# Moving the low parts of gate and up from GpSimd to VectorE in the steps with several token groups

## What is computed

```python
def swiglu(h, w_in, w_out):
    gate, up = jnp.split(h @ w_in, 2, axis=-1)
    return (jax.nn.silu(gate) * up) @ w_out
# x = x + g2 * rms_norm(swiglu(h, ffn_w_in, ffn_w_out), ffn_post_g);  D_FF = 2816
```

## Time and profile before

| | before |
|---|---|
| median of 3 runs | 2308.24 us (2305.38 to 2310.96) |
| the profiled execution's own time | 2305.82 us |
| span of the profile (first to last instruction) | 2304.0 us |
| PE busy | 2247.8 us, 98% of the span |
| DVE busy | 1358.1 us, 59% |
| ACT busy | 865.5 us, 38% |
| POOL busy | 713.5 us, 31% |
| mean granted clock of PE | 0.994 of full speed |

### The profile page before, as it was taken

The page is one execution under the profiler, slowest core; times in us unless marked ns, Lnnn a source line. Parts: engine busy times, 40 slices in busy tenths (PEclk is TensorE's granted clock), DMA queues, the critical chain, the costliest instruction groups (busy, mean ns, idle before and its releaser), DMA issues.

```text
span 2304.0 us, 31766 instructions
## 1 busy us (share of the span) xinstructions
PE 2247.8 (98%) x12964; PEld 2192.4 (95%) x12964; DVE 1358.1 (59%) x2273; ACT 865.5 (38%) x1200; POOL 713.5 (31%) x310
## 2 busy tenths in 40 slices
PE   8999999999999999999999999999999999999998
PEld 4988889999999999999999999999999999999998
DVE  4688864676757656533556668768365244443246
ACT  3577771454211111222343545544434132111234
POOL 3400002453121121332534544542343243221232
PEclk9999999999999999999999999999999999999999
DMA  9322215332323333343343444543343234321323
GB/s 305 104 84 94 94 63 197 120 135 94 126 95 122 99 110 111 125 131 101 110 138 119 150 141 134 178 137 110 101 156 128 74 110 146 110 74 55 101 94 118
DMA packets 211699, 276.13 MB, mean 120 GB/s; under 512 B 4777, under 2 KB 194785, under 8 KB 211041
## 3 DMA queue, kind: packets, MB, share of 16 engines
q1 hardware_dynamic: 183056, 224.36, 29.7%
q10 hardware_dynamic: 26768, 40.30, 5.0%
q0 software_dynamic: 1728, 9.44, 1.0%
HBM read 245.76 MB, written 28.32 MB: 119 GB/s over the span
## 4 chain that ended last, share of the span: by engine, by line
PE 82%; DVE 6%; issue 4%; ACT 3%; POOL 3%; DMA 2%; SPq 0%; ACTq 0%; POOLq 0%; DVEq 0%
PE bank L1011 77%; PE bank L1041 2%; POOL w_lo L2562 1%; DMA raw<-in_l_ffn_w_out 1%; POOL acc L2579 1%; PE bank L1066 1%; DVE mv_lo L2079 1%; DVE y L2042 1%; ACT w_hi L1432 1%; PE bank L1091 1%; DVE pool_sum L2443 1%; DVE hid_lo L2359 0%; DVE wide L2092 0%; DMA mod_stage<-in_l_mod_w 0%; DVE hid L2356 0%
## 5 line engine op out<-in xcount | busy, mean ns | idle before, releaser
L1011 PE MATMUL bank<-mv_hi,w_hi 128*128 128x384 f32 (+2 forms) x2736 | 924.5, 338 | 6.0 <-DVE mv_lo L2174 2.7
L1011 PE MATMUL bank<-mv_lo,w_hi 128*128 128x384 f32 (+2 forms) x2736 | 918.2, 336 | 0.0
L1011 PE MATMUL bank<-mv_hi,w_lo 128*128 128x384 f32 (+2 forms) x2736 | 918.2, 336 | 0.0
L2562 POOL TENSOR_TENSOR w_lo<-raw,w_hi 128x2048 fp32r<-128x2048 f32 x106 | 491.6, 4643 | 1201.5 <-ACT w_hi L1432 1133.2
L1011 PEld LDWEIGHTS bank<-mv_hi,w_hi 128*128 128x128 f32 x2736 | 515.3, 188 | 11.3 <-issue 8.9
L1011 PEld LDWEIGHTS bank<-mv_lo,w_hi 128*128 128x128 f32 x2736 | 515.2, 188 | 0.0
L1011 PEld LDWEIGHTS bank<-mv_hi,w_lo 128*128 128x128 f32 x2736 | 514.8, 188 | 0.0
L1432 ACT ACTIVATE w_hi<-raw 128x2048 fp32r<-128x2048 f32 x159 | 299.4, 1908 | 431.2 <-DMA raw<-in_l_ffn_w_out 237.1
L1011 PE MATMUL bank<-hid_hi,w_hi 128*128 128x384 f32 (+2 forms) x1056 | 361.2, 342 | 13.8 <-DVE hid_lo L2359 12.2
L1011 PE MATMUL bank<-hid_hi,w_lo 128*128 128x384 f32 (+2 forms) x1056 | 356.3, 337 | 0.0
L1011 PE MATMUL bank<-hid_lo,w_hi 128*128 128x384 f32 (+2 forms) x1056 | 356.1, 337 | 0.0
(11 more groups left out here) (156 smaller groups left out, 1837.0 us busy)
## 6 DMA issues: line engine op xcount, KB each, us to landing
raw<-in_l_ffn_w_in SPq DMA_DIRECT2D x92, 1024.0 KB, 5.1
raw<-in_l_ffn_w_out SPq DMA_DIRECT2D x46, 1024.0 KB, 4.9
raw<-in_l_mod_w SPq DMA_DIRECT2D x42, 1024.0 KB, 5.2
residual<-y ACTq DMA_DIRECT2D x10, 1536.0 KB, 7.1
x_old<-residual ACTq DMA_DIRECT2D x10, 1536.0 KB, 7.1
raw<-in_l_w_in SPq DMA_DIRECT2D x8, 1024.0 KB, 5.3
mod_stage<-in_l_mod_w SPq DMA_DIRECT2D x6, 1024.0 KB, 12.1
raw<-in_l_w_out SPq DMA_DIRECT2D x6, 1024.0 KB, 5.1
```

The lines of the kernel that those rows point to most:

```text
L1011: last = pe.matmul(out, w, x, start=start and n == 0, stop=stop and n == len(steps) - 1)
L2562: pool.tensor_tensor(w_lo[:, slot(w), :], raw[:, q % 2, :], w_hi[:, slot(w), :].bitcast(F32), ALU.subtract).then_inc(w_lo_pool, 1)
```

## The change

It edits three places: the list of work, the list of the places of halves, and DVE's program for a step. In a step with several groups that has no case of its own, both low parts of the next step's weights go to DVE: gate's halves behind the adds of m = 5 and m = 7 of the first group, up's behind those of m = 1 and m = 3 of the second. A new list `DOWN_ON_DVE` names the pieces of down whose low part goes to DVE behind the first pair of their step.

```diff
             if own(layer, s) == s:
                 w = WEIGHT["down", layer, s]
                 t += DOWN_LATER if (layer, s) == (0, 0) else 0.0
-                low = ("DVE", 2.2) if w in LAST_SPLITS else ("POOL", SPLIT_LO)
-                work += [("ACT", ("split", w), t, SPLIT_HI), (low[0], ("split", w), t + SPLIT_HI, low[1])]
+                work.append(("ACT", ("split", w), t, SPLIT_HI))
+                if w in DOWN_ON_DVE:
+                    work.append(("DVE", ("split", w), AT["up", PAIR[layer, s, groups[0], 0]] + 2.4, 2.2))
+                elif w in LAST_SPLITS:
+                    work.append(("DVE", ("split", w), t + SPLIT_HI, 2.2))
+                else:
+                    work.append(("POOL", ("split", w), t + SPLIT_HI, SPLIT_LO))
...
-            elif later and len(groups) == 1 and (layer, s) != (0, 0):
-                places[later[1]] = [(groups[-1], 5), (groups[-1], 7)]
+            elif later and (layer, s) != (0, 0):
+                if len(groups) > 1:
+                    places[later[0]] = [(groups[0], 5), (groups[0], 7)]
+                    places[later[1]] = [(groups[1], 1), (groups[1], 3)]
+                else:
+                    places[later[1]] = [(groups[0], 5), (groups[0], 7)]
...
+DOWN_ON_DVE = [WEIGHT["down", layer, s] for layer in range(2) for s in range(len(STEPS[layer]))
+               if own(layer, s) == s and (layer, s) not in STEP_MODS and len(STEPS[layer][s][1]) == NG]
+DOWN_ON_DVE = [w for w in DOWN_ON_DVE if w not in LAST_SPLITS]
...
-ON_DVE = sorted([0, 4, 5, 6, 7, 8, 9, *DVE_SPLITS, *HALVES, *AFTER_POOL, LAST_SPLITS[-1]])
+ON_DVE = sorted([0, 4, 5, 6, 7, 8, 9, *DVE_SPLITS, *HALVES, *AFTER_POOL, *DOWN_ON_DVE, LAST_SPLITS[-1]])
...
                         k = PAIR[layer, s, g, j]
+                        if (g, j, own(layer, s)) == (STEPS[layer][s][1][0], 0, s) and WEIGHT["down", layer, s] in DOWN_ON_DVE:
+                            split(WEIGHT["down", layer, s])
                         if k in SUM_AFTER_PAIR:
```

## The result

Five runs of the changed kernel have a median of 2320.52 us (2316.67 to 2323.89), five of the kernel before, beside them, 2308.89 us (2305.38 to 2310.96). The ratio is 1.005 with a 95% interval of 1.0034 to 1.0065: slower by 11.6 us, where the sum of the forecast was 11.0 (the time put on record was 2318 us, with a range of 2311 to 2326). The profiled execution took 2316.67 us with a span of 2314.9, which is 10.9 us over the span before, at the same mean granted clock, 0.994.

What follows compares the result with a forecast made beforehand. PE's matmuls plus the moments PE stands were taken as the bound, with 82% of the chain of waits. Seven steps at 6.2 us and three with a norm at 4.8 sum to 11.0 us slower: 2318 us, range 2311 to 2326.

Steps and rivals of the forecast that it cites:

- The bank: Out products of the ten steps: a half delays the next add, whose bank PE wants; 0.44 us per costly half.
- quiet step: Seven steps, (0,2) to (0,5), (1,12), (1,19), (1,20), with POOL idle beside the out products: 0.88 us each, 6.2 in all.
- the first late start: At the first half of a step, PE stands 0.33 us for the late add's bank, plus 0.11 of slow restart.
- the second and fourth halves: In each step of the change, these leave the add 0.13 us late, inside the 0.24 allowed: no stall.
- The norm steps: (0,11), (0,16), (1,22), where POOL's sums of squares stretch the halves: 1.6 us a step, 4.8 in all.
- the whole stretch: Upper end for (0,11), (0,16), (1,22): four halves of 1.86 us to the next add, 3.4 us a step, 10.2 in all.
- The rest of the edit: Loads released later, POOL's relief, DVE's added wait: all free; down's load beats ACT's need by 0.9 us.
- The empty list for down: `DOWN_ON_DVE` excludes all six steps with three groups, so it names no piece and down stays on POOL.
- The chains: Norm chains laid out again in following steps; `hid_lo` waits may go or double, -7.8 to +7.8 us, taken as 0.
- Rival 2: Out products of the ten steps: halves are free and POOL's relief counts, leaving a 7.8 us gain, 2300.4; chance 0.04.
- Rival 3: Three steps with a norm: every half at 1.86 us and sums late on PE, 22.4 us in all, 2330; chance 0.12.
- Rival 1: Steps (0,12) to (1,0): norm chains settle better and pay back 7.8 us, 2311.4, no measurable slowdown; chance 0.14.

Runs made afterwards that it cites:

- the up-alone kernel: Changed kernel with gate's low part back on POOL and up's halves behind m = 5 and m = 7 of the last group: 2314.95 us, 1.0029.
- the quarters: Changed kernel with gate's and up's low parts in pieces of 512 columns behind each of eight adds, instead of halves: 2317.69 us, 1.0041.

## Why the prediction was right

**The bank.** Right, and shown: four banks take all of the loss away, with DVE as busy as in the change. The size of a quiet step was forecast at 0.88 us and measured at 0.96 in (0,2), 0.9 to 1.0 in all seven. What was mis-sized is the first late start, 0.43 instead of 0.33: PE started 0.70 us behind the start of the add that it waited for (668.57 less 667.87), where 0.60 had been read, so the slack there was 0.14 and not 0.24. Why is open. Of this 0.03 came back in a quicker restart (0.08 for 0.11); the third half's, 0.34 and 0.11, was met. That the second and fourth halves are free was right.

**The norm steps.** The direction was right, the term a little small: 1.6 us a step was forecast, 2.1, 2.2 and 1.4 are read from late starts, 5.7 for 4.8. All of that is the bank's, for with four banks the out products of these steps take no longer than before; what PE loses behind them is norm work that came earlier and is paid back in part. How the halves meet POOL is seen in the timeline of DVE in (0,11):

```profile
1099.15 1.97 DVE L2129 TENSOR_TENSOR w_lo<-raw,w_hi 128x1024 fp32r<-128x1024 f32 x1
...
1101.99 1.21 DVE L2129 TENSOR_TENSOR w_lo<-raw,w_hi 128x1024 fp32r<-128x1024 f32 x1
...
1104.61 1.67 DVE L2129 TENSOR_TENSOR w_lo<-raw,w_hi 128x1024 fp32r<-128x1024 f32 x1
...
1107.14 1.21 DVE L2129 TENSOR_TENSOR w_lo<-raw,w_hi 128x1024 fp32r<-128x1024 f32 x1
```

POOL adds up squares there from 1097.90 to 1109.24, one sum right behind the other. Two of these sums:

```profile
1099.01 1.03 POOL L2593 TENSOR_TENSOR acc<-acc,wide 128x392 f32<-128x392 f32 x1
...
1104.17 1.03 POOL L2593 TENSOR_TENSOR acc<-acc,wide 128x392 f32<-128x392 f32 x1
```

I had put three halves midway, at 1.5 us to the next add, and a clean fourth. In fact two are stretched and two are clean, though POOL sums beside all four; in (0,16) likewise (2.03 and 1.69 us), and in (1,22) only the third is stretched (1.69). So the mean was about right by luck, and its reason was not: a half isn't stretched by the share of its time in which POOL is busy, it is stretched or it isn't. The times show what decides. A half that begins while a sum runs ends 1.08 us after that sum: the two sums above end at 1100.04 and 1105.20, the halves at 1101.12 and 1106.28. A clean half begins within 0.02 us of a sum's end, and then the sum behind it is the longer one (2.02 and 2.00 us in (0,11)). The row of before had the same 1.08, and in ten of the traces no half that begins beside a running POOL instruction lies more than 0.06 us off this rule. So the two take turns, and the later one waits. The Trainium skill (GPSIMD Engine Reference, Specifications) says that GpSimd's SBUF interfaces are shared with VectorE and that VectorE's work with two SBUF inputs contends. The traces agree, 1.97 us against 1.21; the whole stretch, 10.2 us for the three steps, did not come.

**The rest of the edit.** Down's load went out at 1103.23, 7.4 us later than before, of which 4.1 are the lead that the kernel had lost by then; so 3.3 later, where 3.6 was forecast. With the 4.9 us that a load of `w_out` still takes on the page after, it lands at 1108.1. ACT still waits for PE and not for the load:

```profile
1111.40 1.92 ACT L1444 ACTIVATE w_hi<-raw 128x2048 fp32r<-128x2048 f32 x1 [8.76 <-PE bank L1023]
```

The margin is 3.3 us instead of 0.9, since PE itself came later. The empty list for down was right as well.

**The chains.** I took 0, with 7.8 us on either side. The waits between 1095 and 1460 us after, against the earlier trace rows:

```profile
PE bank L1023 <- DVE hid_lo L2371: 6.1, 3, 2.7
PE bank L1023 <- DVE y L2389: 3.7, 6, 1.0
PE bank L1103 <- POOL acc L2593: 2.7, 2, 2.3
```

For `hid_lo` 1.7 us less, for POOL's sum 0.7 more: near zero, but by luck of the layout. The 3.5 to 6 us that the up-alone kernel lost in (0,13) show that the bounds were not too wide; more than half of what it lost there is the halved clock behind a wait, which the prediction had not priced.

**The rivals.** Rival 2 falls: PE did not find its banks free, and the kernels in which the move costs nothing gain nothing from POOL's relief. The Trainium skill (GPSIMD Engine Reference, Engine selection) would have two-input elementwise work on VectorE; a subtraction is indeed shorter there (2.44 us for two halves against 4.62), and here the move cost 11.6 us, since VectorE's adds are what empties PE's banks. Rival 3 did not come: of the twelve halves of the three steps five were stretched, and PE waited for POOL's sums 8.9 us in all against 8.8. Rival 1 did not come in this change. No kernel here is measurably faster than the one before; several equal it.

## What to carry to other kernels

Before work is put on the engine that empties PSUM, measure the slack of that work: the distance from the start of an eviction to the product that takes its bank, here 0.14 to 0.24 us. If the piece doesn't fit between two evictions, take more banks in turn (four instead of two: 11.6 us to nothing), cut the piece until piece and eviction fit in one product (0.1 us a step instead of 0.9, but only where GpSimd is idle), or put it where the next product wants another bank. And relief of an engine that nobody waits for is no reason for a move.

## What was not expected of the hardware

- A VectorE subtraction and a GpSimd sum take turns, whole instruction by whole instruction. The one that begins while the other runs is stretched, the other isn't: 1.22 us for 1024 columns become 1.67 to 2.03, 0.68 for 512 become 1.02 to 1.47, and a sum of 1.03 becomes 1.86 to 2.02 behind a half and about 1.34 beside the quarters. VectorE's adds, which take one operand from a bank, are not stretched beside the same sums (0.54 to 0.56 us). Finer pieces cost more there: each quarter in step with the sums met one, of four halves one or two did.
- A wait of PE can cost more than its length. Behind 2.88 us in (0,13) of the up-alone kernel the granted clock was 0.50 for 10 us, some 4 us of loss (worked out from matmuls 0.32 us apart instead of 0.17); behind 3.07 us at (1,4) of the kernel before it was 0.50 for 3.4 us. Behind 2.53 us in the same place the changed kernel's stayed at 1.00, yet it fell for 3.4 us behind 2.35 us at 1373.6. So the length of a wait doesn't decide it alone; what does was not tried.
- Between the work on DVE that costs 0.9 us a step and that which costs 5.4 there is only a factor of two in the subtractions. The price of work between adds isn't proportional to it here; it starts at the slack and jumps where the pitch of PE is passed.
